# Feed-forward block of a hybrid decoder layer: block products of Strassen's algorithm in place of plain tile products

## What is computed

```python
D_MODEL, SEQ, DEC_BATCH = 1024, 512, 8          # 520 tokens in all
D_FF = -(-(8 * D_MODEL) // (3 * 256)) * 256     # 2816
...
    x = x.astype(f32) + mix
    hf = rmsnorm(x, g_ffn)
    x = x + (jax.nn.silu(hf @ w_ff1.astype(f32)) * (hf @ w_ff3.astype(f32))) @ w_ff2.astype(f32)
...
    y_prompt = rmsnorm(xp, norm_final_g).astype(x_prompt.dtype)
    y_sample = rmsnorm(xs, norm_final_g).astype(x_sample.dtype)
```

## Time and profile before

| | us |
|---|---|
| median of three runs | 953.78 |
| span of the profiled execution | 952.6 |
| PE busy | 939.6 (99%) |
| DVE busy | 531.5 (56%) |
| ACT busy | 439.3 (46%) |
| POOL busy | 205.1 (22%) |
| first to last matmul of the feed-forward block | 560.9 to 943.6 |

### The profile page before, as it was taken

The page is one execution under the profiler, slowest core; times in us unless marked ns, Lnnn a source line. Parts: engine busy times, 40 slices in busy tenths (PEclk is TensorE's granted clock), DMA queues, the critical chain, the costliest instruction groups (busy, mean ns, idle before and its releaser), DMA issues.

```text
span 952.6 us, 21457 instructions
## 1 busy us (share of the span) xinstructions
PE 939.6 (99%) x8916; PEld 908.4 (95%) x8916; DVE 531.5 (56%) x913; ACT 439.3 (46%) x725; POOL 205.1 (22%) x369
## 2 busy tenths in 40 slices
PE   8999999999999999999999999999999999999997
PEld 4899998999999999999999999999999999999997
DVE  6869985783684487643334655444444444333334
ACT  5469558729828858433323343343332432222221
POOL 6888868542722021000000000000000000000000
PEclk9999999999999999999999999999999999999998
...
GB/s 299 174 79 122 46 185 205 67 286 82 101 217 121 109 151 129 213 126 92 111 111 90 92 86 99 99 80 99 88 88 88 92 98 96 89 95 106 95 60 90
DMA packets 28077, 113.23 MB, mean 119 GB/s; under 512 B 3524, under 2 KB 5620, under 8 KB 26088
## 3 DMA queue, kind: packets, MB, share of 16 engines
...
...
## 4 chain that ended last, share of the span: by engine, by line
PE 83%; POOL 7%; DVE 5%; issue 2%; ACT 2%; DMA 0%; ACTq 0%; DVEq 0%; SPq 0%; POOLq 0%
PE G L1610 67%; PE G L1700 4%; PE Q L1610 3%; POOL pool_tmp L815 3%; PE G L1971 2%; DVE c_samples L1349 1%; PE Q L1758 1%; PE Q L1768 1%; POOL c_abar_packed L818 1%; PE G L1811 1%; POOL u_by_step L975 1%; PE Q L1732 1%; PE Q L1841 1%; DVE x_scaled L1166 1%; DMA x_tokens<-xt 0%
## 5 line engine op out<-in xcount | busy, mean ns | idle before, releaser
L454 ACT ACTIVATE w_high<-raw 128x1024 fp32r<-128x1024 f32 x146 | 154.1, 1059 | 287.7 <-PE G L1610 272.4
L1082 DVE TENSOR_TENSOR w_low<-raw,w_high 128x1024 fp32r<-128x1024 f32 x146 | 181.3, 1245 | 172.1 <-ACT w_high L454 171.5
L1610 PE MATMUL G<-h_high,w_high 128*128 128x256 f32 x1344 | 272.7, 284 | 0.0
L1610 PE MATMUL G<-h_low,w_high 128*128 128x256 f32 x1344 | 270.8, 283 | 0.0
L1610 PE MATMUL G<-h_high,w_low 128*128 128x256 f32 x1344 | 270.7, 283 | 0.0
L1610 PEld LDWEIGHTS G<-h_high,w_high 128*128 128x128 f32 x1344 | 208.4, 188 | 2.1 <-issue 1.6
L1610 PEld LDWEIGHTS G<-h_low,w_high 128*128 128x128 f32 x1344 | 208.4, 188 | 0.0
L1610 PEld LDWEIGHTS G<-h_high,w_low 128*128 128x128 f32 x1344 | 208.3, 188 | 0.0
L1610 PE MATMUL G<-hidden_low,w_high 128*128 128x256 f32 (+1 forms) x308 | 62.0, 283 | 0.0
L1610 PE MATMUL G<-hidden_high,w_high 128*128 128x256 f32 (+1 forms) x308 | 62.0, 283 | 0.0
L1610 PE MATMUL G<-hidden_high,w_low 128*128 128x256 f32 (+1 forms) x308 | 61.7, 281 | 0.0
...
## 6 DMA issues: line engine op xcount, KB each, us to landing
raw<-wst SPq DMA_DIRECT2D x147, 512.0 KB, 3.6
...
```

The costliest lines, as they stand in the source:

```text
L454: return act.activation(out, in_, ACT.Copy, **kw)
L1082: tt(WL[n.slot()][:], raw[n.slot()][:], WH[n.slot()][:].bitcast(F32), ALU.subtract).then_inc(w_lo, 1)
L1610: last = mm(o, w[slot][:, c], h[:, k, c0_:c0_ + width], start=start and x == 0 and t == 0, stop=stop and x == n - 1 and t == 2)
```

## The change

The block is computed as 2x2 block products with seven half-size products in place of eight (Strassen's algorithm, in a form with few additions). The work is cut into 17 **rounds** (`ROUNDS`): the hidden tiles in three groups of 8, 8 and 6, for each of which 4, 4 and 3 "up" rounds compute two hidden tiles each, and then two "down" rounds add the group's part of four output tiles each. That is 11 up rounds and 6 down rounds.

In an up round the weights are four blocks of 128x1024: A11, A12, A21, A22 (two hidden tiles by two halves of the input features, each with both `w_ff1` and `w_ff3`). The activations are split into features' halves and token halves of 260 columns. **Product** i (0 to 6) takes one weight block or sum of blocks and one activation block or sum (`RHS`), held ready in `ffn_in_high`/`ffn_in_low` (for down rounds in `hidden_high`/`hidden_low`, now with seven blocks per pair). A product is 2 sub-units x 4 tiles x 3 terms = 24 matmuls of 260 columns; in the two down rounds of the last group it is 18.

The weight operands are A21+A22, A11, A12, A21+A22-A11, A22-(A21+A22-A11), A12-(A21+A22-A11) and A22. **Four of the seven are made by POOL** (`sum_up`, steps 0 to 3), each by one 128x1024 operation on SBUF; products 0, 3, 4 and 5 wait for them. All seven are then split, high on ACT and low on DVE, where before the same weights were four units with four splits. The split weights have four buffers in place of three, and the split of product q waits for product q-4.

Partial results are added on the way: ACT copies the PSUM results of products 0, 1, 3 and 4, DVE adds those of 2 and 5 to them, POOL adds two more (`c22_ready`) and scales one side by the norm's factor (`b_early`), DVE scales the other (`a_early`) and takes product 6. ACT applies SiLU, DVE multiplies and forms the sums of hidden blocks. In a down round DVE adds 14 results of 260 columns to `x_residual`. The squares of the norm before the block are summed on POOL instead of DVE. At the end the norm is done for one token half and then for the other; DVE scales 5 of the 8 output tiles and POOL 3, with two operations each.

```diff
...
-DOWN_CUT = (0, 8, 15, 22)
+DOWN_CUT = (0, 8, 16, 22)
 N_UNITS = N_DOWN + 3 * KC
 assert N_UNITS % RING == 0
+
+
+
+HALF = T // 2
+PAIRS_OF = tuple((b - a) // 2 for a, b in zip(DOWN_CUT, DOWN_CUT[1:]))
+ROUNDS = tuple(r for g, n in enumerate(PAIRS_OF) for r in [("up", g, p) for p in range(n)] + [("down", g, p) for p in range(2)])
+NR = len(ROUNDS)
+UNITS_R = 7
+RHS = (2, 0, 6, 4, 3, 1, 5)
...
+        def w_at(q):
+
+            return 3 if q % 4 == 0 else (N_FF + q % 4 - 1) % RING
...
+        def round_source(r, i):
+
+            return (FB[r % 2], BB, DB, FB[r % 2], BB, FB[r % 2], EB[r % 2])[i]
...
+            for r in range(1, NR):
+                before = N_FF + UNITS_R * (r - 1)
+                if r == 1:
+                    sp.wait_ge(w_lo, N_FF)
+                else:
+                    sp.wait_ge(w_lo, before - UNITS_R + 6)
+                load_a21(r)
+                if r >= 2:
+                    sp.wait_ge(w_lo, before - UNITS_R + 7)
+                load_a22(r)
+                sp.wait_ge(w_lo, before + 5)
+                load_a11(r)
+                sp.wait_ge(sums, 4 * (r - 1) + 4)
+                load_a12(r)
...
+            def split_high(q):
+
+                r, i = divmod(q, UNITS_R)
+                if q >= 4:
+                    act.wait_ge(su_done, 2 * (q - 4) + 2)
+                if i == 0 or 3 <= i < 6:
+                    act.wait_ge(sums, 4 * r + (1, 0, 0, 2, 3, 4)[i])
+                elif i == 1:
+                    act.wait_ge(a11_in, 16 * r + 16)
+                elif i == 2:
+                    act.wait_ge(a12_in, 16 * r + 16)
+                else:
+                    act.wait_ge(a22_in[r % 2], 16 * (r // 2) + 16)
+                copy(halves_of(WH[w_at(q)], r), halves_of(round_source(r, i), r)).then_inc(w_hi, 1)
...
+            def up_round(r):
+                u, x, k = up_index(r), bank_x(r), hid_at(r)
+
+                def take(i, bank, slot, s):
+                    for su, (t, o) in enumerate(((G, DT[:, slot, :]), (Q, CB[:, min(slot, 3), :]))):
+                        act.wait_ge(su_done, 2 * (UNITS_R * r + i) + su + 1)
+                        copy(o, t[:, bank, 0:HALF]).then_inc(s, 1)
+
...
+                if u > 0:
+                    act.wait_ge(hidl_ready, 2 * u - 1)
+                take(0, 2, 2, took_z0)
+                next_high(0)
+                take(1, x, 1, took_x1)
+                next_high(1)
+                next_high(2)
...
+                take(3, x, 0, took_x3)
+                next_high(3)
+                if u > 0:
+                    act.wait_ge(hidl_ready, 2 * u)
+                take(4, x, 7, took_x4)
+                next_high(4)
+                next_high(5)
+                act.wait_ge(a_early, u + 1)
+                act.activation(DT[:, 0:3, :], DT[:, 0:3, :], ACT.Silu).then_inc(silu_done, 1)
+                act.wait_ge(took_x6, 2 * r + 1)
+                act.activation(DT[:, 7, :], DT[:, 7, :], ACT.Silu).then_inc(silu_done, 1)
+                next_high(6)
+                act.wait_ge(hid_ready, 2 * u + 1)
+                copy(HIDH[:, 0:5, k, :], DT[:, 1:6, :]).then_inc(hidh_ready, 1)
+                act.wait_ge(hid_ready, 2 * u + 2)
+                copy(HIDH[:, 5:7, k, :], DT[:, 6:8, :]).then_inc(hidh_ready, 1)
...
+            def sum_up(r, step):
+
+                f, b, d, e = (halves_of(x, r) for x in (FB[r % 2], BB, DB, EB[r % 2]))
+                unit = N_FF + UNITS_R * r
+                if step == 0:
+                    pool.wait_ge(a21_in[r % 2], 16 * (r // 2) + 16)
+                    pool.wait_ge(a22_in[r % 2], 16 * (r // 2) + 16)
+                    tt(f, f, e, ALU.add).then_inc(sums, 1)
+                elif step == 1:
+                    pool.wait_ge(a11_in, 16 * r + 16)
+                    pool.wait_ge(w_lo, unit + 1)
+                    tt(f, f, b, ALU.subtract).then_inc(sums, 1)
+                elif step == 2:
+                    pool.wait_ge(sums, 4 * r + 2)
+                    pool.wait_ge(w_lo, unit + 2)
+                    tt(b, e, f, ALU.subtract).then_inc(sums, 1)
+                else:
+                    pool.wait_ge(sums, 4 * r + 3)
+                    pool.wait_ge(a12_in, 16 * r + 16)
+                    pool.wait_ge(w_lo, unit + 4)
+                    tt(f, d, f, ALU.subtract).then_inc(sums, 1)
...
+            for r, (kind, _, _) in enumerate(ROUNDS):
+                u = up_index(r)
+                sum_up(r, 2)
+                sum_up(r, 3)
+                if r < NR - 1:
+                    sum_up(r + 1, 0)
+                    sum_up(r + 1, 1)
+                if kind == "up":
+                    for su, (p5, u3) in enumerate(((DT[:, 2, :], DT[:, 7, :]), (CB[:, 2, :], CB[:, 3, :]))):
+                        pool.wait_ge(took_z0, 2 * r + su + 1)
+                        pool.wait_ge(took_x4, 2 * r + su + 1)
+                        tt(p5, p5, u3, ALU.add).then_inc(c22_ready, 1)
...
+                    pool.wait_ge(c22_ready, 2 * u + 2)
+                    pool.wait_ge(took_y2, 2 * r + 2)
+                    pool.wait_ge(took_z5, 2 * r + 2)
+                    tt(CB[:, 0:3, :], CB[:, 0:3, :], frq[:, 0:3, :], ALU.mult).then_inc(b_early, 1)
...
+            for count, half in enumerate((1, 0)):
+                pool.wait_ge(inverse_copied, count + 1)
+                for m in range(5, KC):
+                    own.do(tt(X1[:, m, (H0, H1)[half]], X1[:, m, (H0, H1)[half]], inv_sb[:, half, :], ALU.mult))
+                    pool.tensor_scalar(X1[:, m, (H0, H1)[half]], X1[:, m, (H0, H1)[half]], g_fin[:, m:m + 1], None, ALU.mult).then_inc(y_pool, 1)
...
+            def split_low(q):
+
+                r, i = divmod(q, UNITS_R)
+                dve.wait_ge(w_hi, N_FF + q + 1)
+                tt(halves_of(WL[w_at(q)], r), halves_of(round_source(r, i), r), halves_of(WH[w_at(q)], r).bitcast(F32),
+                   ALU.subtract).then_inc(w_lo, 1)
...
+            def up_round(r):
+                u, x, k = up_index(r), bank_x(r), hid_at(r)
+                C = (DT, CB)
+                next_low(r, 0)
+                next_low(r, 1)
+                for su, t in enumerate((G, Q)):
+                    product_done(r, 2, su)
+                    dve.wait_ge(took_x1, 2 * r + su + 1)
+                    tt(C[su][:, 1, :], t[:, 1, 0:HALF], C[su][:, 1, :], ALU.add).then_inc(took_y2, 1)
+                next_low(r, 2)
...
+                next_low(r, 3)
+                next_low(r, 4)
+                for su, t in enumerate((G, Q)):
+                    product_done(r, 5, su)
+                    dve.wait_ge(took_x3, 2 * r + su + 1)
+                    tt(C[su][:, 0, :], t[:, 2, 0:HALF], C[su][:, 0, :], ALU.add).then_inc(took_z5, 1)
+                dve.wait_ge(c22_ready, 2 * u + 1)
+                dve.wait_ge(took_y2, 2 * r + 1)
+                dve.wait_ge(took_z5, 2 * r + 1)
+                tt(DT[:, 0:3, :], DT[:, 0:3, :], frq[:, 0:3, :], ALU.mult).then_inc(a_early, 1)
+                next_low(r, 5)
+                product_done(r, 6, 0)
+                tt(DT[:, 7, :], G[:, x, 0:HALF], frq[:, 3, :], ALU.mult).then_inc(took_x6, 1)
+                product_done(r, 6, 1)
+                dve.wait_ge(c22_ready, 2 * u + 2)
+                tt(CB[:, 3, :], Q[:, x, 0:HALF], frq[:, 3, :], ALU.mult).then_inc(took_x6, 1)
+                dve.wait_ge(silu_done, 2 * u + 1)
+                dve.wait_ge(b_early, u + 1)
+                own.do(tt(DT[:, 0:3, :], DT[:, 0:3, :], CB[:, 0:3, :], ALU.mult))
+                own.do(tt(DT[:, 3:5, :], DT[:, 0:3:2, :], DT[:, 1::-1, :], ALU.subtract))
+                tt(DT[:, 5, :], DT[:, 2, :], DT[:, 3, :], ALU.subtract).then_inc(hid_ready, 1)
+                dve.wait_ge(silu_done, 2 * u + 2)
+                dve.wait_ge(took_x6, 2 * r + 2)
+                own.do(tt(DT[:, 7, :], DT[:, 7, :], CB[:, 3, :], ALU.mult))
+                dve.wait_ge(hid_ready, 2 * u + 1)
+                tt(DT[:, 6, :], DT[:, 7, :], DT[:, 5, :], ALU.subtract).then_inc(hid_ready, 1)
+                next_low(r, 6)
+                dve.wait_ge(hidh_ready, 2 * u + 1)
+                tt(HIDL[:, 0:5, k, :], DT[:, 1:6, :], HIDH[:, 0:5, k, :].bitcast(F32), ALU.subtract).then_inc(hidl_ready, 1)
+                dve.wait_ge(hidh_ready, 2 * u + 2)
+                tt(HIDL[:, 5:7, k, :], DT[:, 6:8, :], HIDH[:, 5:7, k, :].bitcast(F32), ALU.subtract).then_inc(hidl_ready, 1)
...
+            def part_product(r, i, su, ks, start, stop, ready=None, at=None):
+
+                q = UNITS_R * r + i
+                hi, lo = (BH, BL) if ROUNDS[r][0] == "up" else (HIDH, HIDL)
+                bank = {0: 2, 2: 1, 5: 2}.get(i, bank_x(r))
+                s = w_at(q)
+                for k in ks:
...
+                    c = slice(512 * su + P * k, 512 * su + P * k + P)
+                    for t, (w, h) in enumerate(((WH, hi), (WH, lo), (WL, hi))):
+                        last = mm((G, Q)[su][:, bank, 0:HALF], w[s][:, c], h[:, RHS[i], k, :],
```

(3 more changed lines are left out.)

573 lines of the change are left out of this document (354 added, 219 removed).

## The result

The changed kernel takes 1012.4 us in the median of 4 runs (1010.2 to 1014.2), the kernel before 954.5 in the runs beside it: a ratio of 1.061, 95% interval 1.059 to 1.063. The direction was forecast and the size was not: 988 was predicted, and 1012.4 lies just above the stated range of 932 to 1012 (the prediction's own upper terms added up to 1013). Medians here are of runs in a kernel's usual state; one run of the kernel "sums on DVE, later" took 1133.9 us at a granted clock of 0.74 and is left out of its median. The profiled execution has a span of 1011.7 us, 59.1 more than before.

What follows compares the result with a forecast made beforehand. PE's matmuls were taken to bound the kernel before. From 953.8 us: -47.6 for removed matmuls, +74.8 for DVE/POOL turns in 11 up rounds, +7 for entry and exit, giving 988; range 932 to 1012.

Steps and rivals of the forecast that it cites:

- the prediction's own upper terms: Whole kernel: up rounds of 28.7 us without overlap at changes, plus upper entry and exit costs; together 1013 us.
- What bounded the kernel before, and the matmuls removed: Feed-forward stage: PE's matmuls bound it; 396 fewer, 2772 left, save 47.6 us; a full round needs 20.2 us of PE.
- DVE and POOL take turns; the up round is 27.0 us: Up rounds: DVE with two SBUF inputs and POOL reading SBUF exclude each other; 27.0 us against PE's 20.2, eleven times.
- the walk: One up round followed operation by operation in code order, 0.15 us off at each DVE/POOL change; ends at 27.0 us.
- The lower bound: Up round: 24.2 us, with POOL sums of 2.1 us and perfect packing; 953 us in total without entry cost.
- Which step of PE waits: Up round: PE stands before product 4, waiting for `w_lo`, for 6.8 us.
- Entry, 2 us (0 to 6): Output projection's last four steps: added DVE and POOL work costs 2 us; products 0 and 1 need no late activations.
- Down rounds stay with PE, 20.2: Down rounds: DVE with POOL's four sums takes 19.4 us, under PE's 20.2, so no extra cost.
- Exit, 5 us (3 to 7): Last matmul to end of span: POOL scaling three tiles per half makes 14.4 us of 9.3, 5 more.
- Rival (c), the clock: Up rounds: PE's stops before product 4 let its clock fall, 32 us more, 1020 in total; chance 0.07.
- (a): Up rounds: DVE/POOL turns don't bind, PE stays the bound; 913 us in total; chance 0.13.
- (b): Up rounds: turns bind, but sums near 2 us fall under DVE's idle spots; 22 to 23.5 a round, 933 to 950; chance 0.10.

Runs made afterwards that it cites:

- sums on DVE, later: Changed kernel with later weight sums, small additions and second 780-element scaling on DVE, three of four sums behind `hidden_low`; 1008.6 us, ratio 1.0543.

## Why the prediction was right in direction and short in size

- **What bounded the kernel before, and the matmuls removed:** right. The stage has 2772 product matmuls, and where nothing waits a full round takes 20.1 us against the 20.2 of the sum.
- **DVE and POOL take turns; the up round is 27.0 us:** right for the seven up rounds that follow another (26.5 us on DVE, 26.2 in the mean on PE), and shown by an experiment that kept POOL as busy without reading. DVE's own 17.1 us are 17.1 in the trace, and the 9.9 that the walk adds for POOL are 8.9 and 9.5 in two rounds. The sum was taken at 2.4 us and took 2.40 alone, 2.50 in the mean of `L1253`. The sums on POOL cost 71 us, some 50 of them by their turns. The lower bound rested on sums of 2.1 us, a slip: by the slope of 1.9 that it names, 1.33 for 512 elements makes 2.3 for 1024. The Trainium skill (GPSIMD Engine Reference, section "3.1 Elementwise — side-by-side cycle accounting") has 4497 ns for 2048 elements, which made an estimate of 2.25; the trace has a little more.
- **Which step of PE waits:** wrong. It isn't product 4 for `w_lo` but product 3 for a bank, by way of ACT and `hidl_ready`. In the changed kernel's steady rounds it makes no difference, since the period is DVE's own. With the sums on DVE this loop was the round.
- **Entry, 2 us (0 to 6):** failed. The stage began 1.2 us late and the first two rounds took 8.9 more than 27.0 each: 10.1 where 2 stood. The cause is the early sums, which stand in POOL's queue behind the operand sums and in turn with DVE: with them cut the total falls by 9.3. With zeroing in place of the sums the two rounds give back 5.1, with sums of one column another 8.6, so the queue weighs more there than the turns. I had let products 0 and 1 off and not followed products 2 to 4, and I had left out the reciprocal.
- **Down rounds stay with PE, 20.2:** the step that failed, and the largest miss. It was right for the second of each pair in the first two groups (20.9, 21.0), wrong for the first (31.0, 30.9) and for both short ones of the last group (25.1, 18.9, where 15.1 stood): 36.9 us more in all, where the forecast had nothing. In the first of a pair PE's last quarter of products 0 to 2 waits for `hidden_low`, up to 4.8 us, and the take for another 2.6. I had added up rounds one by one and not looked at the change from the one kind to the other, where the last hidden tiles have no further up round to hide behind. Against that, the up round behind a down round takes 20.1 on PE, not 27.0; with the steady rounds' 26.2 that is 19.1 less. In the second group the two nearly cancel (+2.1), in the last they don't (+6.0), and the first group has no such up round to set against it. The rounds behind the entry thus missed by 17.8 net and the entry by 8. That the total missed by no more than 24 is in part luck: two of the nine up rounds, priced at 27.0, hid 14 us of it. The two versions with seven products in the down rounds alone show the cause at the group's end: with the takes and splits put in order there the three first down rounds lost 9.4 us. How the 36.9 divide between turns, order and clock wasn't tested.
- **Exit, 5 us (3 to 7):** 5.8 measured, in range. 3.6 came back by the medians with DVE scaling all tiles, 2.0 by profiles at the same clock level.
- **Rival (c), the clock:** it did fall behind the stops, by up to 2.8 us in an up round, 27.5 us of slower pitch in all, where the rival had 32. I had thought it unlikely for want of a row. It cost little in steady up rounds, where keeping it up left the period as it was. The tail is 3.1 us longer at the lower level. What the clock costs in the entry and in the first down rounds isn't separated.
- **Rivals (a) and (b):** refuted, since the sums took what the line said and the turns bound.
